# Decay factors of a gated recurrence: level-by-level products of the forget factors in place of exponentials of tree sums, on one Trainium2 core

## The reference, cut to what matters

```python
z = f_pre                                   # (S, 8, 128)
logf = log_sigmoid(z) + log1p(lb * exp(-z)) # = log(lb + (1 - lb) * sigmoid(z))
k = (1 - lb) * sigmoid(-z)                  # = 1 - f
b = cumsum(logf)
decay = exp(min(b[t] - b[s], 0)) * tri      # per key channel
A[t, s] = sum_d q[t, d] * decay[t, s, d] * k[s, d]
o[t] = sum_s A[t, s] v[s] + (q[t] * exp(b[t])) state
o = o * rsqrt(mean(o * o) + eps)            # per head
y = o * gain * silu(gate);  out = y @ w_out
```

## Time and profile before

| | |
|---|---|
| median of three runs | 1033.12 us (1032.94 to 1034.14) |
| span of the profiled execution | 1031.7 us, first to last instruction |
| PE busy | 1019.3 us, 99% |
| DVE busy, ACT busy, POOL busy | 730.5 us (71%), 654.4 us (63%), 11.3 us |
| mean granted TensorE clock | 0.998 |
| memory | 167.54 MB, 162 GB/s |
| chain that ended last | PE 86%, ACT 5%, DVE 4%, DMA 3% |

### The profile page before, as it was taken

How to read it: one execution, slowest core, us unless ns; L and a number is a source line. 1 busy time by engine, 2 the same in 40 slices (tenths; PEclk the granted TensorE clock), 3 DMA queues, 4 the chain that set the end, 5 groups by cost and what they waited for, 6 DMA issues and landing times.

```text
span 1031.7 us, 19279 instructions
## 1 busy us (share of the span) xinstructions
PE 1019.3 (99%) x8170; PEld 912.9 (88%) x8170; DVE 730.5 (71%) x1070; ACT 654.4 (63%) x911; POOL 11.3 (1%) x15
## 2 busy tenths in 40 slices
PE   9999999999999999999999999999999999999997
PEld 7899987888989999988999998888799999988875
DVE  5774688875656888765565657978875656699686
ACT  7677667564465565644466678767755657676683
POOL 0000000000000000000000000100000000001000
PEclk9999999999999999999999999999999999999999
DMA  8852454476547655566554543423665455344231
GB/s 292 300 195 83 144 164 145 161 232 207 174 153 232 187 164 188 191 216 189 168 159 122 174 143 109 157 84 104 192 199 167 134 163 164 101 140 149 84 105 61
DMA packets 97431, 167.54 MB, mean 162 GB/s; under 512 B 6913, under 2 KB 32257, under 8 KB 96833
## 3 DMA queue, kind: packets, MB, share of 16 engines
q1 hardware_dynamic: 95792, 159.18, 48.7%
q0 software_dynamic: 1120, 5.51, 1.5%
q10 hardware_dynamic: 432, 1.62, 0.4%
HBM read 165.23 MB, written 1.05 MB: 161 GB/s over the span
## 4 chain that ended last, share of the span: by engine, by line
PE 86%; ACT 5%; DVE 4%; DMA 3%; issue 2%; SPq 0%; DVEq 0%; ACTq 0%
PE proj L625 13%; PE proj L627 12%; PE proj L626 12%; PE proj L634 12%; PE proj L636 12%; PE proj L635 12%; DMA raw<-in_w_in 2%; DVE wlo L1587 1%; DMA raw<-in_w_mem_kv 1%; ACT whi L1110 1%; PE mix L955 1%; PE mix L956 1%; PE mix L695 1%; PE mix L987 1%; PE mix L670 1%
## 5 line engine op out<-in xcount | busy, mean ns | idle before, releaser
L1587 DVE TENSOR_TENSOR wlo<-raw,whi 128x1024 fp32r<-128x1024 f32 (+2 forms) x304 | 355.0, 1199 | 140.2 <-ACT whi L1110 138.3
L1110 ACT ACTIVATE whi<-raw 128x1024 fp32r<-128x1024 f32 (+2 forms) x304 | 305.8, 1038 | 147.8 <-PE proj L636 63.3
L625 PE MATMUL proj<-act_hi,whi 128*128 128x256 f32 x1064 | 303.5, 285 | 0.9 <-ACT arena L1388 0.5
L627 PE MATMUL proj<-act_hi,wlo 128*128 128x256 f32 x1064 | 301.0, 283 | 0.0
L626 PE MATMUL proj<-act_lo,whi 128*128 128x256 f32 x1064 | 300.9, 283 | 0.0
L625 PEld LDWEIGHTS proj<-act_hi,whi 128*128 128x128 f32 x1064 | 203.1, 191 | 3.9 <-ACT arena L1388 1.4
L626 PEld LDWEIGHTS proj<-act_lo,whi 128*128 128x128 f32 x1064 | 203.2, 191 | 0.9
L627 PEld LDWEIGHTS proj<-act_hi,wlo 128*128 128x128 f32 x1064 | 203.2, 191 | 0.2
L634 PE MATMUL proj<-whi,y_hi 128*128 128x512 f32 (+1 forms) x340 | 134.9, 397 | 0.8 <-DVE y_lo L2099 0.4
L635 PE MATMUL proj<-wlo,y_hi 128*128 128x512 f32 (+1 forms) x340 | 131.7, 387 | 0.0
L636 PE MATMUL proj<-whi,y_lo 128*128 128x512 f32 (+1 forms) x340 | 131.7, 387 | 0.0
(11 more groups left out here) (360 smaller groups left out, 1232.7 us busy)
## 6 DMA issues: line engine op xcount, KB each, us to landing
raw<-in_w_in SPq DMA_DIRECT2D x144, 512.0 KB, 4.5
raw<-in_w_up SPq DMA_DIRECT2D x88, 256.0 KB, 4.3
raw<-in_w_out SPq DMA_DIRECT2D x32, 512.0 KB, 4.2
raw<-in_w_down SPq DMA_DIRECT2D x22, 512.0 KB, 4.8
raw<-in_w_mem_k SPq DMA_DIRECT2D x8, 512.0 KB, 4.1
raw<-in_w_o SPq DMA_DIRECT2D x8, 512.0 KB, 4.0
raw<-in_w_mem_v SPq DMA_DIRECT2D x8, 512.0 KB, 4.3
raw<-in_w_mem_kv SPq DMA_DIRECT2D x7, 512.0 KB, 6.4
```

The costliest lines, as they stand in the source:

```text
L625: mm(o, wh[:, i, wc], hi[:, k0 + i, :], start=begin and j % 2 == 0, stop=False, skip_group_check=True)
L627: last = mm(o, wl[:, i, wc], hi[:, k0 + i, :], start=False, stop=end, skip_group_check=True)
L1110: fn(whi[c % SPLIT][:, 0:w], raw[c % SLOTS][:, 0:w], ACT.Copy).then_inc(s.w_hi, 1)
L1587: tt(wlo[c % SPLIT][:, 0:w], raw[c % SLOTS][:, 0:w], f32(whi[c % SPLIT][:, 0:w]), ALU.subtract).then_inc(s.w_lo, 1)
```

## The change

Logarithms, the tree of sums and their exponentials go. The forget factor f itself is made (FORGET; in layer 1 as sigmoid times (1 - lb) plus lb). Keys HKT and a copy of the queries HQP (already multiplied with f once) are multiplied in place, for all heads, by the forgets of the neighbouring half block, level after level from half size 1 to 64 (`grow`), and before each step PE makes the products of the level (`products(l)`, now for all eight heads). GpSimd makes the products of the forgets of whole blocks (TOTAL[2] to TOTAL[64]). The outputs of all heads come at once at the end, in one group hgo behind mlaout1.

```diff
-    groups[at:] = [("mlaout0", mlaout[0]), ("hgo0", []), ("hgg0", hg["hgg0"]), ("hgo1", []), ("hgg1", hg["hgg1"]), ("hgo2", []),
-                   ("mlaout1", mlaout[1])]
+    groups[at:] = [("mlaout0", mlaout[0]), ("hgg0", hg["hgg0"]), ("hgg1", hg["hgg1"]), ("mlaout1", mlaout[1]), ("hgo", [])]
...
 # GpSimd
-                pool.wait_ge(s.hg_z, 8 * L + 1)
-                nc.gpsimd.memset(arena[:, 0:3584], 0.0).then_inc(s.hg_zero, 1)
+                pool.wait_ge(s.hg_f, L + 1)
+                pool.wait_ge(s.mla_tk, 8 * L + 8)
+                pool.wait_ge(s.mla_s, 2 * L + 2)
+                for n, half in enumerate((2, 4, 8, 16, 32, 64)):
+                    if n:
+                        pool.wait_ge(s.hg_g, 6 * L + n)
+                    parts = TOTAL[half // 2].rearrange("p (n s) -> p n s", s=2)
+                    nc.gpsimd.tensor_tensor(TOTAL[half], parts[:, :, 0], parts[:, :, 1], ALU.mult).then_inc(s.hg_g, 1)
+                    if half == 4:
+                        pool.wait_ge(s.hg_x, 8 * L + 8)
+                        nc.gpsimd.memset(arena[:, 0:3584], 0.0).then_inc(s.hg_zero, 1)
...
 # PE, behind values(LV, LPT[1], ...)
                 pe.wait_ge(s.mla_yl, L + 1)
                 project("mlaout0", L, y_hi, y_lo, 8, part=(0, 1))
+                pe.wait_ge(*out_of("hgq1", L))
+                products(8)
+                products(7)
                 pe.wait_ge(*stage(4, L))
                 project("mlaout0", L, y_hi, y_lo, 8, part=(1, 2))
+                products(6)
                 project("hgi1", L, act_hi, act_lo, part=(3, 4))
+                gates(0)
+                products(5)
+                gates(1)
+                products(4)
+                gates(2)
+                gates(3)
+                products(3)
+                gates(4)
+                products(2)
+                gates(5)
+                products(1)
+                gates(6)
+                gates(7)
+                products(0)
+                for half in range(2):
+                    pe.wait_ge(*out_of(f"hgi{half}", L))
+                pe.wait_ge(s.hg_at, L + 1)
+                pe.wait_ge(s.hg_ca, 6 * L + 4)
+                g = place[L, "hgo"]
+                pe.wait_ge(evac[g % 2], g // 2)
+                for p in range(4):
+                    outputs_within(p)
+                for p in range(4):
+                    outputs_across(p)
+                project("mlaout1", L, y_hi, y_lo, 8, part=(0, 1))
+                squares(0)
+                squares(1)
                 project("mlaout1", L, y_hi, y_lo, 8, part=(1, 2))
                 squares(2)
-                outputs(3)
-                project("hgout0", L, y_hi, y_lo, ready=y_ready, part=(0, 1))
                 squares(3)
-                project("hgout0", L, y_hi, y_lo, ready=y_ready, part=(1, 3))
+                project("hgout0", L, y_hi, y_lo, ready=y_ready, part=(0, 3))
...
 # ACT, behind leave("hgq1", ...)
+                act.wait_ge(s.hg_n, L + 1)
+                if L:
+                    fn(HF, HF, ACT.Exp)
+                    fn(HT, HT, ACT.Exp).then_inc(s.hg_s, 1)
+                else:
+                    fn(FORGET, HT, ACT.Exp).then_inc(s.hg_f, 1)
                 split_until(ahead_of("hgi0", L, 1))
                 shares(1)
...
 # ACT, the end of the recurrence
+                leave_only("hgg1", L, HGT[:, 4:8, :], ACT.Silu)
+                leave_128()
                 nc.scalar.preload_act_table(ACT.Ln)
+                for p in range(4):
+                    square(p)
                 split_until(ahead_of("mlaout1", L, 0))
+                logs(0)
+                logs(1)
+                roots(0)
+                split_until(ahead_of("mlaout1", L, 1))
                 rounded(0)
                 rounded(1)
+                nc.scalar.preload_act_table(ACT.Ln)
+                logs(2)
+                logs(3)
+                split_until(ahead_of("hgout0", L, 0))
+                roots(2)
                 rounded(2)
                 rounded(3)
...
 # DVE
+                for half, l, name, n in ((1, 7, "mlaout0", 1), (2, 6, "hgi1", 3), (4, 5, "hgg0", 0), (8, 4, "hgg0", 1),
+                                         (16, 3, "hgg0", 3), (32, 2, "hgg1", 0), (64, 1, "hgg1", 1)):
+                    for four in range(2):
+                        grow(half, four)
+                    if half == 1:
+                        masked(8)
+                    if l >= 3:
+                        masked(l)
+                    if half == 4:
+                        dve.wait_ge(*done("mlaout0", L))
+                        tt(X[:, :, 0:512], bank("mlaout0", L), X[:, :, 0:512], ALU.add).then_inc(out_of("mlaout0", L)[0], 1)
+                    split_until(ahead_of(name, L, n))
+                    if half == 16:
+                        diagonal()
...
+                gated(0)
+                gated(1)
+                dve.wait_ge(s.hg_w, 4 * L + 2)
+                nc.vector.memset(stat[:, 240:241], 0.0).then_inc(out_of("hgo", L)[0], 1)
+                split_until(ahead_of("mlaout1", L, 0))
                 gated(2)
+                gated(3)
                 scaled(0)
+                scaled(1)
                 lower(0)
+                split_until(ahead_of("mlaout1", L, 1))
+                lower(1)
+                scaled(2)
+                scaled(3)
                 dve.wait_ge(*done("mlaout1", L))
                 tt(X[:, :, 512:1024], bank("mlaout1", L), X[:, :, 512:1024], ALU.add).then_inc(out_of("mlaout1", L)[0], 1)
```

More of the change, by code:

```diff
@@ L1074, in layer @@
-                outputs(2)
-                products(UNITS - 1)
+                pe.wait_ge(s.mla_yl, L + 1)
+                project("mlaout0", L, y_hi, y_lo, 8, part=(0, 1))
+                pe.wait_ge(*out_of("hgq1", L))
+                products(8)
+                products(7)
+                pe.wait_ge(*stage(4, L))
+                project("mlaout0", L, y_hi, y_lo, 8, part=(1, 2))
+                products(6)
+                project("hgi1", L, act_hi, act_lo, part=(3, 4))
+                gates(0)
@@ L1234, in _ @@
             split_until(ahead_of("sbv", None, 1))
-            act.wait_ge(s.tree_in, 16)
-            fn(tree[:, :, :, :].rearrange("p b l t -> p (b l t)"), TREE_IN, ACT.Copy).then_inc(s.tree_ok, 1)
             act.wait_ge(s.lb_a, 1)
@@ new lines, in leave_32, with leave_64 @@
+                def leave_32():
+                    act.wait_ge(s.hg_zero, L + 1)
+                    act.wait_ge(s.hg_pr, 18 * L + 14)
+                    for n in range(2):
+                        rows = slice(64 * n, 64 * n + 32)
+                        src = mix[rows, LEVEL_BANK[2], :].rearrange("p (h b t) -> p h b t", h=HG_H, b=NB)
+                        fn(both(AT[rows, :, 64 * n + 32:64 * n + 64], HG_H, 32), src, ACT.Copy).then_inc(s.hg_ca, 1)
+                def leave_64():
+                    for four in range(2):
+                        act.wait_ge(s.hg_pr, 18 * L + 15 + four)
+                        src = mix[0:64, four, :].rearrange("p (h b t) -> p h b t", h=4, b=NB)
+                        fn(both(AT[0:64, 4 * four:4 * four + 4, 64:P], 4, 64), src, ACT.Copy).then_inc(s.hg_ca, 1)
@@ L1491, in rounded, with roots @@
+                def roots(p):
+                    act.wait_ge(s.hg_sc, 4 * L + p + 2)
+                    v = HKT[:, 2 * p:2 * p + 4, :]
+                    fn(v, v, ACT.Exp, scale=-0.5).then_inc(s.hg_r, 2)
                 def rounded(p):
@@ L1494, in rounded @@
                     fn(pair_of(y_hi, p), pair_of(HQT, p), ACT.Copy).then_inc(s.hg_yh, 1)
-                def logs(dst, src):
-                    return fn(dst, src, ACT.Ln, bias=epsb[:, 0:1], scale=1.0 / HG_D)
-                def roots(dst):
-                    return fn(dst, dst, ACT.Exp, scale=-0.5)
-                log_forget(0)
+                keys()
                 latent_out(1)
                 split_until(ahead_of("hgi1", L, 2))
-                weights(0, 0, 2)
-                log_forget(1)
@@ L1541, in layer @@
-                act.wait_ge(*out_of("hgo1", L))
-                link(logs(HKT[:, 0:4, :], HKT[:, 0:4, :]))
-                roots(HKT[:, 0:4, :]).then_inc(s.hg_r, 2)
-                square(2)
+                for n in range(4):
+                    split_until(ahead_of("hgg0", L, n))
+                leave_only("hgg0", L, HGT[:, 0:4, :], ACT.Silu)
+                split_until(ahead_of("hgg1", L, 0))
+                leave_32()
+                split_until(ahead_of("hgg1", L, 1))
+                leave_64()
@@ L2016, in layer @@
                 split_until(ahead_of("hgi0", L, 0))
-                for j in range(HG_H):
-                    last = ts(HL[:, j, :], HF[:, j, :], cur[:, 4 + j:5 + j], 0.0, ALU.subtract, ALU.min)
-                link(last)
+                if L:
+                    dve.wait_ge(s.hg_s, L)
+                    for j in range(HG_H):
+                        last = stt(FORGET[:, j, :], HF[:, j, :], cur[:, 4 + j:5 + j], HT[:, j, :], ALU.mult, ALU.add)
```

(12 more changed lines are left out.)

456 lines of the change are left out of this document (141 added, 315 removed).

## The result

The changed kernel takes 1039.25 us, the median of 1040.03, 1038.58, 1038.22 and 1039.92, against 1033.24 us of four runs of the kernel before beside it: ratio 1.0053, 95% interval 1.0041 to 1.0065. It is slower by half a percent. The forecast was 1032.6 us, no change, with 1038 us as the upper end.

The account below looks back on a forecast made before the run. PE, busy 1019.3 of 1031.7 us, was taken as the bound. PE work -30.4, waits +25.7 and clock +5.0 gave +0.3 us; walked in time order -1.3, middle -0.5: 1032.6 us, no change, range 1021 to 1038.

Parts of the forecast that it names:

- PE work less: PE in both layers: tree sums and logarithm transposes go, products cost slightly more; net 15.2 us a layer less.
- wait 1: Ahead of gates(0), PE waits for hgi1's last piece to leave PSUM: about 1.35 us a layer (1.2 to 1.6).
- wait 2: At the first grow, PE waits for DVE's chain from values on: 0.5 us a layer (0 to 1.5).
- wait 3: Ahead of products(1), half size 64, PE waits for DVE's mask, weights, diagonal and grow: 1.7 us a layer (0.5 to 3.5).
- wait 4: In the tail, hgout0 waits until DVE adds mlaout1 to X, behind ACT's roots: 9.1 us a layer (7 to 11).
- the clock behind it: PE's clock after each layer's tail wait of 9 us: 2.5 us per wait (1.5 to 3.5), 5 us in all.
- layer 1 alone, the longer exponentials: Layer 1: ACT's 2048-element exponentials delay the second attention group's shares, longer keys the first grow: 1.3 us (0 to 3).
- GpSimd's block products: Products of whole blocks' forgets on GpSimd come 20 us ahead of need, so put at nothing.
- rival A: Waits are smaller: tail 4 to 5 us, the clock may hold, 11 to 12 us off, 1021 us; 18%.
- What is hidden: ACT's, DVE's and the tree load's savings count nothing beside PE; GpSimd's memset and block products are ready early enough.
- Rival B: GpSimd's multiplications hold up DVE: 1.5 to 3 us on layer 1's shares, 1 us each first grow; 1037 us; 22%.
- the same matmuls in another order: PE's products, regrouped by level: 64 products of 32 columns (128 instructions) take 1.22 us; packing 1.3 us a layer more.

Follow-up runs that it names:

- the base: The changed kernel itself, unedited, run again on the chip of the experiments: 1039.95 us, ratio 1.0053.
- group order: Changed kernel with hgo before mlaout1 in the list of PSUM groups, so hgout0 follows hgo on its bank: 1031.88 us, ratio 0.9976.
- filler: Changed kernel with 38 plain 128 x 128 matmuls from constants filling PE's tail wait in each layer: 1034.59 us, ratio 1.0008.
- products apart: Changed kernel with mlaout0's second piece between products(8) and products(7), and hgi1's last piece ahead of products(6): 1035.92 us, ratio 1.0016.
- woven alone: Changed kernel with a quarter of a level's products behind each quarter of a projection piece, nothing else edited: 1044.71 us, ratio 1.0102.
- half woven: Changed kernel with hgo before mlaout1, GpSimd's products later, tail reordered, only products(7) woven into mlaout0, products(6) after hgi1, three masks later: 1012.40 us, ratio 0.9788.
- the first probe: Changed kernel with 320 more 32-column matmuls on one output in each layer's tail wait: 1054.80 us.
- the second probe: Changed kernel with 192 more matmuls in each layer's tail wait, going round four column groups and sixteen output columns: 1038.59 us, ratio 1.0041.

## Why the prediction was wrong

The direction of every large term was right, the sum was not: two costs of the changed kernel were not in it, and some waits were put too high. Each term over both layers, in us, as put and as found:

| step of the prediction | put | found |
|---|---|---|
| PE work less | -30.4 | -23.0 busy, with some 9 of half clock in it: about -32 |
| wait 1, hgi1's evacuation | 2.7 | 2.2 |
| wait 2, first grow | 1.0 | 0.2 |
| wait 3, products(1) | 3.4 | 0.3 |
| wait 4, the tail | 18.2 | 18.6 |
| the clock behind it | 5.0 | 4.7 |
| layer 1 alone, the longer exponentials | 1.3 | 0.3 (left when GpSimd is out of the way) |
| GpSimd's block products | 0 | 5.2 |
| stalls for instructions | 0 | 5.5, and about 1.7 of clock in layer 1 |

**PE work.** The sums and turnings are gone as put. The busy time holds the half clocks: 4.7 us of the tails, 1.35 us of layer 1's transposes (twelve took 2.82 us behind their wait, 1.47 in the earlier trace rows), about 1.7 us behind a stall of layer 1, and 1.5 us early in the program (below). Without these it fell by about 32. The further 2 us may be the changes of kind that the sums brought, at 0.13 us each; the forecast counted only blocks. That was not tried.

**Waits 1 and 4** came as the rows gave them: 1.11 us for 1.35, 9.31 us for 9.1. Program order on ACT plus its table loads gave the tail to 2%, and rival A is out.

**The clock.** The 5.0 us were the author's estimate, and no row of the kernel before shows the term: in the earlier trace rows the clock falls behind PE's last work, with no pass after it, and beside the slow first passes of the earlier trace rows it reads 1.00. The runs showed 4.7 us in its place, 12 passes 0.43 us apart behind each wait of 9.31 us. Rival A let the clock hold behind a shorter wait: it fell in one of 4.45 us and held in one of 1.74; between the two it did both (see the last section).

**Wait 3.** The mask was right (0.7 put, 0.74 found), a diagonal copy was put at 0.6 us and took 0.43, and DVE's lead was larger than the 1 us allowed. **Wait 2** was small by luck, not for the reason given: the first grow takes 4.2 us, not 2.4, and the stall of 2.4 us inside products(7) gave DVE the time.

**The step that failed first** is "What is hidden": the block products were put at nothing because they are early enough. How early they are was the wrong question; what they do to their neighbours costs 5.2 us. Rival B had it, with 22%, with the right place in layer 1 and the right size there (1.5 to 3 us; 2.7 found, and 1.35 of clock behind it); of its second place the splits were right (0.4 to 0.6 us a layer longer), the first grow was not. Its condition, that VectorE's operations on two SBUF operands stand still beside GpSimd's multiplications, is borne out by the shares (2.22 us against 0.69) and the splits (3.90 us for three against 3.49).

**The second** is "the same matmuls in another order", at 1.22 us for 128 instructions. The earlier trace rows shows one such block with projections and sums about it; two back to back were never in the trace. The kernel before had 1.4 us of "issue" in its waits, one of them 1.22 us inside a block of 128, and the forecast passed over that row. This was in no rival, and it is why the time lies above the range: 1032.6 + 5.2 + 5.5 + 1.7, less the 5.4 us that waits 1, 2 and 3 and layer 1 were put too high, is 1039.6; measured 1039.25. The 2 us that PE's work fell further and the 1.5 us of half clock early in the program, both left out of this sum, nearly cancel. That the sum meets the time to 0.4 us is luck in part: the 5.2 us have 2 to 3 us of doubt, and the stalls and the clock behind them differ by as much from one profile to the next.

**Open.** The profiled execution of the changed kernel has a half clock from 178 to 182 us too, far ahead of the change, worth 1.5 us; so have the profiles of its second run as the base and of five variants (group order, filler, products apart, woven alone, half woven); those of the other six and of the kernel before have not. It may explain part of the spread of the runs, as the stalls may; what sets it off was not found.

## What to carry to other kernels

When a list of small matmuls is regrouped into longer runs, count the instructions as well as the time: 256 passes of 10 ns in a row stalled here for 2.0 to 3.2 us at one place, and blocks of 128 with one projection piece between them still for 0.2 to 2.4; yet mixing them finely with projections cost 0.26 us for each pair of changes, so break only the longest run. Work moved to an idle GpSimd was free here only where nobody waited for VectorE; starting it behind shares(1), or moving it into VectorE's own gap, gave the same 5 us. And an accumulation bank freed late cost twice here, the wait (9.31 us a layer) and the half clock behind it (2.4 us): the edits of order in the tail gave 18.5 of the 23.7 us, by difference (23.7 less the 5.2 of GpSimd's place; they were not run by themselves).

## What the hardware showed unasked

- TensorE's instructions came in packets of 256 (63 packets for the 16,084 of the changed kernel, 10 more for the 2,560 of the first probe, 6 more for the 1,536 of the second). With passes at 10 ns the stalls ended 4.01 us apart in the second probe, 3.5 to 4.6 in layer 1's products(7).
- Going from projection passes to 32-column products and back took TensorE 0.26 us (three passes and 32 small ones: 1.28 us in place of 1.02).
- Passes of 32 columns that follow each other on one output stood 32 ns apart (640 in 20.45 us), in turn on the four column groups and other outputs 10 ns (128 in 1.3 us).
- VectorE's in-place multiplication of 1024 elements whose sides alternate element by element took 2.1 us; those with longer runs took 1.18.
- The granted clock fell in or behind waits of 9.31, 4.45, 3.34 and 3.21 us, and stayed up behind those of 1.74. Between them the same wait did both: behind the 2.69 us ahead of layer 1's transposes it fell in the changed kernel and stayed up in the variant with the products further apart, where the twelve took 1.53 us; behind layer 0's stall it fell for 2.34 us in the base's profile and stayed up for 2.36 in the first one. The length of the wait alone does not tell which.

```profile
923.55 1.53 PE L912 MATMUL mix<-const,arena 128*128 128x128 f32 x12 [2.69 <-DVE arena L1918]
```
